# Delta rule's output stage: the gate projections one head earlier in TensorE's order

## What is computed

```python
def rms_norm(x, g):
    xf = x.astype(F32)
    y = xf * lax.rsqrt(jnp.mean(xf * xf, axis=-1, keepdims=True) + EPS)
    return (y * g.astype(F32)).astype(x.dtype)

def finish(o_pair, gate, dtype):
    o = rms_norm(o_pair[0] + o_pair[1], norm_g)
    o = o.reshape(*o.shape[:2], GDN_HEADS * GDN_DV) * jax.nn.silu(gate.astype(F32))
    return o.astype(dtype) @ w_out
```

## Time and profile before

| what | us |
|---|---|
| median of 3 runs | 3908.39 |
| lowest and highest of them | 3907.4, 3918.83 |
| the profiled execution's own time | 3908.51 |
| its span in the trace | 3906.6 |
| TensorE busy with matmuls | 3685.6 (94%) |
| VectorE busy | 1934.1 (50%) |
| ScalarE busy | 1516.5 (39%) |
| GpSimd busy | 844.9 (22%) |
| DMA, mean over the span | 77 GB/s |

### The profile page before, as it was taken

How to read it: one execution, slowest core, us unless ns; L and a number is a source line. 1 busy time by engine, 2 the same in 40 slices (tenths; PEclk the granted TensorE clock), 3 DMA queues, 4 the chain that set the end, 5 groups by cost and what they waited for, 6 DMA issues and landing times.

```text
span 3906.6 us, 60691 instructions
## 1 busy us (share of the span) xinstructions
PE 3685.6 (94%) x25542; PEld 3020.1 (77%) x25542; DVE 1934.1 (50%) x2996; ACT 1516.5 (39%) x2548; POOL 844.9 (22%) x842
## 2 busy tenths in 40 slices
PE   7989898999999999998999999999999899999998
PEld 4678887987888757786888788876777688878887
DVE  5556565535544565645343543446565533454343
ACT  5533233323323356645233432234575522343222
POOL 1222122121211132442110120203244311002120
PEclk7989999989999899998999999999999899999999
DMA  6310030012222202111223122221111022222222
GB/s 235 123 44 3 13 71 8 3 55 103 98 97 97 70 28 76 60 65 38 97 97 133 67 97 97 96 83 38 60 60 66 33 97 97 103 92 97 97 97 87
DMA packets 81542, 300.86 MB, mean 77 GB/s; under 512 B 8824, under 2 KB 9976, under 8 KB 80504
## 3 DMA queue, kind: packets, MB, share of 16 engines
q1 hardware_dynamic: 80240, 294.90, 21.6%
q10 hardware_dynamic: 1032, 2.10, 0.5%
HBM read 292.76 MB, written 4.19 MB: 76 GB/s over the span
## 4 chain that ended last, share of the span: by engine, by line
PE 75%; DVE 10%; ACT 6%; issue 5%; POOL 3%; DMA 1%; SPq 0%; DVEq 0%; POOLq 0%; ACTq 0%
PE ps L208 74%; DVE wlo L239 1%; DVE he L247 1%; ACT whi L227 1%; PE ps L213 1%; DVE ac L247 1%; ACT ha L227 1%; POOL p L243 1%; DVE hc L2448 1%; ACT L227 1%; DVE ss L247 1%; ACT wp L228 1%; DVE ws L247 1%; DVE ha L239 1%; DVE sml L1919 0%
## 5 line engine op out<-in xcount | busy, mean ns | idle before, releaser
L239 DVE TENSOR_TENSOR wlo<-wraw,whi 128x1024 fp32r<-128x1024 f32 x537 | 690.0, 1289 | 778.9 <-ACT whi L227 778.2
L208 PE MATMUL ps<-hh,whi 128*128 128x512 f32 x1840 | 729.3, 396 | 8.6 <-DVE hl L239 4.6
L208 PE MATMUL ps<-hl,whi 128*128 128x512 f32 x1840 | 721.3, 392 | 0.0
L208 PE MATMUL ps<-hh,wlo 128*128 128x512 f32 x1840 | 721.0, 392 | 0.0
L227 ACT ACTIVATE whi<-wraw 128x1024 fp32r<-128x1024 f32 x537 | 559.7, 1049 | 214.4 <-PE ps L208 176.7
L208 PEld LDWEIGHTS ps<-hh,whi 128*128 128x128 f32 x1840 | 348.1, 189 | 90.5 <-ACT hh L227 7.0
L208 PEld LDWEIGHTS ps<-hh,wlo 128*128 128x128 f32 x1840 | 348.2, 189 | 73.9
L208 PEld LDWEIGHTS ps<-hl,whi 128*128 128x128 f32 x1840 | 348.3, 189 | 70.2
L208 PE MATMUL ps<-u,u 64*64 64x64 f32 (+2 forms) x6016 | 228.5, 228 | 25.5 <-DVE u L239 16.9
L208 PEld LDWEIGHTS ps<-u,u 64*64 64x64 f32 (+1 forms) x6016 | 209.1, 139 | 42.5 <-DVE u L239 18.5
L239 POOL TENSOR_TENSOR sml<-sml,con 128x4 f32<-128x4 f32 (+3 forms) x36 | 66.5, 1848 | 647.3 <-DVE sml L244 584.7
(11 more groups left out here) (400 smaller groups left out, 7035.4 us busy)
## 6 DMA issues: line engine op xcount, KB each, us to landing
wraw<-weights SPq DMA_DIRECT2D x537, 512.0 KB, 3.2
x<-xT SPq DMA_DIRECT2D x2, 2048.0 KB, 9.4
bias_lines<-ln ACTq DMA_DIRECT2D x1, 2048.0 KB
xmf<-memT SPq DMA_DIRECT2D x2, 1024.0 KB, 4.6
out<-x SPq DMA_DIRECT2D x4, 512.0 KB, 2.6
bias<-bias_lines SPq DMA_DIRECT2D x1, 1536.0 KB, 9.3
con<-consts SPq DMA_DIRECT2D x1, 1379.0 KB, 17.1
ctxt<-ctxT SPq DMA_DIRECT2D x1, 1024.0 KB, 18.8
```

Source lines behind the costliest of these rows:

```text
L208: self.last, self.open = self.e.matmul(out, lhsT, rhs, start=start, stop=stop, skip_group_check=skip), True
L239: return self.e.tensor_tensor(out, a, b, op)
```

## The change

`pe_gout` gets a helper `gate(h)` that holds head h's projection. The projection of head 0 is put ahead of the sums of squares, and in the loop the projection of head h+1 is put ahead of head h's spread. In `dve_gout` the first feed, `dve_feed("og", 0)`, is called once more ahead of the wait for the sums; the call in the loop then finds nothing left to do for head 0. ScalarE's and GpSimd's orders are as they were, and so are the sums, the spreads, the projections and the blocks.

```diff
     def pe_gout(self):
         K, pe = self, self.pe
+
+        def gate(h):
+            K.proj(("og", h), K.wkey(3072 + h * 128), [(K.ps.take(pe, "og", h), K.lat)])
+
+        gate(0)
         b = K.ps.take(pe, "osum")
         for h in ks8:
             pe.wait_ge(K.act.at("osq", h) if h % 2 else K.dve.at("osq", h))
...
         sm = K.sml["o",]
         for h in ks8:
-            bg, br = K.ps.take(pe, "og", h), K.ps.take(pe, "or", h)
-            K.proj(("og", h), K.wkey(3072 + h * 128), [(bg, K.lat)])
+            if h < 7:
+                gate(h + 1)
+            br = K.ps.take(pe, "or", h)
             pe.wait_ge(K.pool.at("oroot"))
...
         dve.wait_ge(K.ended("scan", 1))
         for h in range(0, 8, 2):
             dve.tt(K.OSQ[:, h, :], K.OT[:, h, :], K.OT[:, h, :], ALU.mult).then_inc(dve("osq", h), 1)
+        K.dve_feed("og", 0)
         sm = K.sml.take(dve, "o")
         dve.wait_ge(pe.at("osum"))
```

## The result

The changed kernel took 3940.47 us (median of 4 runs, 3934.11 to 3943.47), the kernel before beside it 3907.89 us (4 runs): ratio 1.0072, 95% interval 1.0056 to 1.0088. It is slower, inside the range that was forecast and 6.9 us over the forecast value. (A ratio in this document, with its interval, rests on the single runs and is not the quotient of the two medians beside it, which would be 1.0083 here.) In a later comparison with more runs it took 3939.6 us beside 3914.64 for the kernel before, ratio 1.0067 (1.005 to 1.0084): 25.0 us more.

What follows compares the result with a forecast made beforehand. TensorE, carrying 75% of the chain of waits, was taken to bound the kernel. 3908.5 less 2.9 (front) plus 21.0 (loop and end) plus 7 (clock falls) gave 3933.6 us, range 3922 to 3942.

Steps and rivals of the forecast that it cites:

- The loop: Gates 2 to 7: TensorE stands 2.8 us in each for a late weight block; a period takes 9.15 us, before 6.36.
- The end: Output projection 0 waits for a block, then `ylo`, and ends at 906.7 against 888.6 us before.
- The clock in the loop: Behind seven stalls TensorE's clock falls, each fall costing 2.0 us, half of it absorbed: 7 us, ends 0 and 23.
- the terms of the sum, 21.0 and 7: Loop and end without clock falls cost 21.0 us; the clock falls behind the stalls cost 7 us.
- The front: Start of the stage, gate 0 ahead of the sums, gate 1 ahead of spread 0: a gain of 2.9 us.
- The root: Ahead of spread 0: gate 1, taking 8.15 us, hides the scaling and GpSimd's power, done 6.6 us after the sums' end.
- The sum: Whole kernel: 3908.5 - 2.9 + 21.0 + 7 = 3933.6 us, 0.64% more, with ends 3922.7 and 3953.6.
- the stalls leave the clock alone: Rival, in the loop: the stalls come but the clock stays up, 3926.6 us; chance 0.20.
- the loop settles at half clock: Rival: the whole loop runs at half clock, a period takes 12.5 us, 3949 us in all; chance 0.10.
- the block isn't late: Rival, middle of gate 2: the block is ready in time, only the front's gain remains, 3905 us; chance 0.06.

Runs made afterwards that it cites:

- The feeds' experiments: Changed kernel with the loop's weight blocks converted one block further ahead, by ScalarE and VectorE (3913.82 us) or by ScalarE alone (3915.69 us); kernel before 3913.1 us.
- the stalls filled: Changed kernel with 12 extra useless matmuls in the middle of gates 2 to 7: 3929.47 us, kernel before 3914.64 us, ratio 1.0042.
- the second profile: The changed kernel, unaltered, run and profiled again: 3939.6 us, kernel before 3914.64 us, ratio 1.0067.
- the kernel with the loop alone: Changed kernel with the sums put back ahead of gate 0, only the loop's order changed: 3941.15 us, kernel before 3914.64 us, ratio 1.0071.
- Woven in: Against the kernel before: gate 0 first, sums spread among gate 1's pieces, gate 2 ahead of spread 0, feeds further ahead: 3910.93 us, ratio 0.9999.
- the old feeds: Kernel before with gates 0 and 1 ahead of spread 0 and the feeds left where they were: 3906.69 us, ratio 0.9989.

## Why the prediction was right

**The loop.** Right in mechanism, place and size. I had 2.8 us in each of gates 2 to 7; there are six waits of 2.7. A period at full clock was to be 9.15 us and is 9.34: in such a one TensorE restarted 5.41 us after "on" began (854.61 to 860.02) where I had 5.33, and the gate's second half took 2.84 us where I had 2.72. The feeds' experiments show that the wait is for the block and for its place in ScalarE's order.

**The end.** Right but for the clock. By the forecast's times two waits stand in output projection 0, 1.7 us for the block and 2.5 for `ylo`; they are 1.8 and 2.4. A fall of the clock behind the second was not in the forecast; it costs 1.6 us in output projection 1. The row "issue" hid the first one, and only VectorE's timeline names it.

**The clock in the loop.** Right in sign and, partly by luck, nearly in size: 7 us forecast, 5.8 measured between the spreads. I had counted a fall for each of seven stalls, at 2.0 us with half of it absorbed. In fact four of the six stalls in the loop had one and the seventh had none, and nothing was absorbed: half clock began as TensorE restarted and lay in the gate's second half, and such a period was 1.3 to 1.6 us longer than one without. Too many falls and too low a price for each nearly cancel. The table in the Trainium skill, TensorE: Matmul & The Clock Gate, "Why this matters for your kernels", by which idle gaps of this length would cost no clock, is not borne out here: 2.7 us was enough in four cases of six, with dense matmuls on both sides.

**Loop, end and clock together.** From the point where gates 0 and 1 and one spread are done to the end of output projection 0 it was 45.16 us before (843.44 to 888.60) and 73.19 after (843.44 to 916.63): 28.0 more, where the terms of the sum, 21.0 and 7, make 28.0. That they agree to a tenth is chance. With the stalls filled the same stretch took 67.9 us (840.37 to 908.23), 22.7 over before, and 0.5 of that is the last fall of the clock. So the loop and the end without the clock cost 22.2 us, 1.2 more than forecast, and the falls between the spreads, with 5.8, 1.2 less.

**The front.** Right in kind, too small. I had 2.9 us of gain; in the profiled execution it is 6.1 (29.85 us from the scan's end to head 1's spread before, 23.77 for the same work after). There the scan happened to end at full clock, and gate 0 took 5.6 us instead of 8.15. In the second profile, where the scan ended at half clock, the gain is 4.3. The sums were to take 9.8 us from start to start and took 10.5, and gate 1 behind them 7.0 instead of 8.15. The root was covered, as said. That the earlier `dve_feed` is worth nothing by itself was not tried.

**The sum.** By these pieces the stage costs 22.0 us in one profile and 23.7 in the other, output projection 1 adds 1.6 in both, and the kernel lost 25.0 us in the comparison with most runs (forecast 25.1). The first comparison's 32.6 us between the medians is larger mainly because its four runs of the kernel before fell low: their median is 3907.89, and those of the later comparisons, of 15 to 35 runs, are 3913.1 to 3914.86. The rest of the program, the same in both, varies by 14 us between the profiles. I gave too little room for that: a forecast of 25 us has to stand against two medians that each move by several microseconds.

**The rivals.** That the stalls leave the clock alone fell with the filled stalls. That the loop settles at half clock fell with the windows: after each fall in the changed kernel the level was back within 3 to 4 us; only the kernel with the loop alone had a longer one, from 876.3 until after 882, in its period of 11.8. That the block isn't late fell with the six waits.

## What to carry to other kernels

When an instruction is moved earlier on the engine that bounds, look at what its operands' producers have queued in front of them: here a weight block's conversion stood behind a head's work on two other engines, and the move took away the work that had covered that chain. Price the chain link by link from the timeline against the work left between; with that, each of the six stalls was known to a tenth of a microsecond. And where several engines hand one item around in a loop, compare the loop's period with the bounding engine's: with 5.8 against 6.4 us one delay shrank so slowly that 4.9 us of waiting were left at the end of eight heads.

## What the runs showed of the hardware

- One-column matmuls keep TensorE busy by every count in the profile and let its clock fall all the same (from 828 to 838 in the changed kernel, the later sums and the start of gate 1: busy 10.00 of 10 us, clock 0.53, after 1.00 from 825 to 828, where the sums began). Woven in, four of them ahead of every three dense ones, they did not: 12 us at 1.00.
- An idle stretch of 2.7 us between dense matmuls lowered the clock in four of six cases in both profiles of the changed kernel and in five of six with the loop alone; filled with useless matmuls, in none. The single wait of 1.85 us in gate 2, with the old feeds, had no fall behind it, and those of 4.7 to 4.9 us for `ylo` all had.
- Single executions of the same program on one core spread over 20 us (3899.42 to 3919.5 in 35 runs), half a per cent. Part of it can be seen as the clock: the scan ahead of the stage ended at full clock in three of the fourteen profiles and at half in the others, worth about 1.8 us in gate 0. Whether that is all of it was not tried.
